# Second mixture of experts: gate and up rows dealt to the partitions in fours

## The chip, the cores and the metric

One core of one Trainium2 chip runs the whole program in one launch. The metric is the device time of one execution in microseconds (us). Beside it stands the time of one profiled execution, whose trace is read here.

## The reference, cut to what matters

The program runs two stacks of blocks over 256 tokens of 1024 features in float32. The second stack has two layers, and each ends in the mixture that this change touches (`hier_moe`, inputs whose names end in `_2`). It has 16 experts in 4 groups of 4. Every token chooses one group and two experts in it:

```python
a = silu(einsum('td,edf->tef', t, w_gate)) * einsum('td,edf->tef', t, w_up)   # d = 1024, f = 256
y = einsum('tef,efd->td', a * comb[:, :, None], w_down)
```

`w_gate` and `w_up` of an expert are 1024 x 256 (1 MB each, rows of 1 KB), `w_down` is 256 x 1024 (rows of 4 KB). The 48 MB of weights of a layer are read once. The sum over d may be taken in any order, as long as weights and tokens use the same one.

## The kernel before, in words

**Stages.** The first stack (with a larger mixture, `od_moe_gu` and `od_moe_down`) takes about the first two thirds of the span. Then come, for each layer of the second stack, an attention mixer and the mixture. Everything is written out by hand: each engine has one program in order, and semaphores join them.

**Blocks.** Weights come in blocks of 2 MB through a ring of seven slots (`ring`, 16 KB in each partition). SyncE issues the transfers (line 1258, in `load`), in the order of a list of blocks. Before it loads block i + 7 into a slot, it waits until TensorE has read block i (`free_slot`). For the second mixtures it also waits for the ranking of the four groups by their number of tokens (`order_ready`, line 1301), since the group that a block belongs to is chosen at run time.

**Order in a layer.** A group is two pairs of experts, c0 and c1. Each pair needs a gate block, an up block and a down block; a gate block holds the gate weights of two experts side by side, loaded by two DMAs of 1 MB. The 24 blocks of a layer are numbered here b0 to b23: gate and up of pair 0 (b0, b1), gate and up of pair 1 (b2, b3), down of pair 0 (b4); then for each further group gate and up of its c0, the down block of the group before, gate and up of its c1, down of its c0; at the end the last down block. So the gate and up blocks of the third group's second pair are b14 and b15, those of the fourth group b17, b18 and b20, b21, and the last two down blocks b22 and b23.

**Layout.** A slot holds a gate block as eight chunks of 512 columns: chunk k has row 128 k + p of both experts in partition p, 256 columns of each. So every run that a DMA moves is one row, 1 KB. A down block has rows of 1024, so its runs are 4 KB.

**Tokens.** For each layer TensorE turns the normalised tokens into rows (line 1974), ScalarE copies the four results into `xn_tok` (line 2630), and TensorE gathers the tokens of each group out of it, 128 features at a time (line 2002), into `x_group`.

**Products.** Groups are ranked by tokens. The two largest are computed in tiles of 32 rows, four at a time (`triple_one`, `triple_two`, `triple_three`; the matmuls are in `tile_stream`, line 1752), down products at line 1856. The two smaller ones are computed in tiles of 64 rows (`group_pair`, line 1806; `group_down`, line 1819). A transpose of the hidden values (lines 1842 and 1730) stands in the middle of the next product, and the scatter back to the tokens (lines 1914 and 1916) behind it. The moving operand of gate and up matmuls is a chunk of 512 columns out of the ring, the stationary one 32 or 64 tokens of `x_group`.

Where a group has more tokens than its tiles hold (96 in the first two, 64 in the others), a branch (lines 1308, 2051) computes the rest. It did not run here.

Of the kernel before, what the change touches and what calls it, by code (L numbers as in the profile page):

```python
# [30 lines left out]
P = 128  # L31
# [3 lines left out]
KD = D // P  # L35
# [9 lines left out]
E2, E2_FF = 16, 256  # L45
# [49 lines left out]


GROUP_CAP = 3 * QP
GROUP_CAPS = [GROUP_CAP, GROUP_CAP, HP, HP]
GROUP_MOST = [T, T // 2, T // 3, T // 4]
GROUP_MORE = [(g, at, min(P, n - at + 1 & ~1)) for g, (n, cap) in enumerate(zip(GROUP_MOST, GROUP_CAPS)) for at in range(cap, n, P)]  # L100
# [113 lines left out]
def stacked_blocks_kernel(nc, A, consts_dram, counts_dram, slots_dram, out):  # L214
    with ExitStack() as ctx:
# [297 lines left out]
        def slot_data(b):  # L513

            return ring[:, b.slot, :] if b.slot < SLOTS else zf

        def kblk(b):

# [456 lines left out]
        def experts(l, h_at):  # L975
# [20 lines left out]
            st.loads = []  # L996

            def by_group(W):
                return W[l].rearrange("(g e) (k p) n -> g e p k n", e=EPG, p=P)

            def pair(W, n):

                return [(lambda j: lambda b: lambda g: (kblk(b)[:, :, j * E2_FF:(j + 1) * E2_FF],
                                                        by_group(W)[g, 2 * n + j]))(j) for j in range(2)]

            def gate_up(x, c):
                n = c.c - 2 * x.i
# [232 lines left out]
        @block_.sync  # L1240
        def _(sp):
            def released(b):
                if b.release is not None:
                    sp.wait_ge(*b.release)
                for tile in b.other_tiles:
                    sp.wait_ge(*tile)

            def free_slot(i):

                if blocks[i].earlier is not None:  # L1250
                    released(blocks[i].earlier)

            def load(i, expert=None):
                b = blocks[i]
                for l in b.loads:
                    place = l(b)
                    dst, src = place if isinstance(place, tuple) else place(expert)
                    sp.dma_start(dst, src).then_inc(slot_landed[b.slot], 16)

            sp.dma_start(x_tok[:, 0, :], A["x"][0][0:P, :]).then_inc(tokens_landed, 16)  # L1260
            for dst, src in SMALL[:ROWS_BY_SP]:
                sp.dma_start(dst, src).then_inc(rows_landed, 16)
            for i in range(SLOTS):
                load(i)
            for dst, src in LATE:
                sp.dma_start(dst, src).then_inc(late_landed, 16)
            for i in range(SLOTS, moe1_first):
                free_slot(i)
                load(i)
            for i in range(*moe1[0].blocks):  # L1270
                free_slot(i)
                load(i, 0)
            sp.wait_ge(order_ready, 1)
            for st in moe1[1:]:
                expert = sp.value_load(order[0:1, st.rank:st.rank + 1], min_val=0, max_val=E1 - 1)
                for i in range(*st.blocks):
                    free_slot(i)
                    load(i, expert)

            sp.wait_ge(excess_ready, 1)  # L1280
            with sp.If(sp.value_load(order[0:1, E1:E1 + 1], min_val=0, max_val=T) > CAPS[0]):
                for b in blocks[moe1_last - SLOTS - 1:moe1_last]:
                    released(b)
                for m, (rank, at, w) in enumerate(MORE):
                    expert = sp.value_load(order[0:1, rank:rank + 1], min_val=0, max_val=E1 - 1)
                    with sp.Fori(0, N1) as s:
                        sp.wait_ge(more_down, s + (m * N1 + 1))
                        for slot_i, src in enumerate((gu1_steps[expert, 0, s], gu1_steps[expert, 1, s], dn1_steps[expert, s])):
                            dst = (ring[:, slot_i, :].rearrange("p (k n) -> p k n", n=WBLK if slot_i < 2 else D))
                            sp.dma_start(dst, src).then_inc(more_landed, 16)  # L1290
                sp.wait_ge(more_added, 4 * len(MORE))
            at = moe1_last
            for st in moe2:
                group = None
                for i in range(at, st.blocks_end):
                    if i == moe1_last + 1:
                        sp.wait_ge(spread_ready, twin.spread + 1)
                    if i == moe2[0].blocks_end + 2:
                        sp.wait_ge(spread_ready, od2.norm.spread + 1)
                    if i == st.blocks_begin:  # L1300
                        sp.wait_ge(order_ready, st.route.order + 1)
                        group = [sp.value_load(order2[0:1, st.l * EG + g:st.l * EG + g + 1], min_val=0, max_val=EG - 1)
                                 for g in range(EG)]
                    free_slot(i)
                    load(i, group[blocks[i].group] if i >= st.blocks_begin else None)
                at = st.blocks_end
                sp.wait_ge(most_ready, st.route.most + 1)
                with sp.If(sp.value_load(most2[0:1, st.l:st.l + 1], min_val=0, max_val=T) > GROUP_CAP):
                    for b in blocks[at - SLOTS:at]:
                        released(b)  # L1310
                    for m, (g, at_slot, w) in enumerate(GROUP_MORE):
                        of = sp.value_load(order2[0:1, st.l * EG + g:st.l * EG + g + 1], min_val=0, max_val=EG - 1)
                        for n in range(2):
                            if n:
                                sp.wait_ge(excess_product[st.l], 9 * m + 5)
                            elif m:
                                sp.wait_ge(excess_product[st.l], 9 * m - 1)
                            for slot_i, W in enumerate((A["moe_w_gate_2"], A["moe_w_up_2"])):
                                dst = ring[:, slot_i, :].rearrange("p (k n) -> p k n", k=KD)
                                for j in range(2):  # L1320
                                    src = st.by_group(W)[of, 2 * n + j]
                                    sp.dma_start(dst[:, :, j * E2_FF:(j + 1) * E2_FF], src).then_inc(excess_landed[st.l], 16)
                            sp.dma_start(ring[:, 2, :].rearrange("p (k n) -> p k n", n=D), st.down_rows[of, n])\
                                .then_inc(excess_landed[st.l], 16)
                    sp.wait_ge(excess_made[st.l], 5 * len(GROUP_MORE))
            for i in range(at, len(blocks)):
                free_slot(i)
                load(i)
            sp.wait_ge(rows_out[1], 2)
            sp.dma_start(out[0][P:2 * P, :], x_tok[:, 1, :]).then_inc(out_landed, 16)  # L1330
            sp.wait_ge(out_landed, 32)
# [12 lines left out]
        def _(pe):  # L1344
# [404 lines left out]

            def tile_stream(f, j, at, b, k, src=xn):  # L1750

                return nc.tensor.matmul(PSB[f.b][j * QP:(j + 1) * QP, :], src[:, k, at:at + QP], kblk(b)[:, k, :],  # L1752
                                        start=k == 0, stop=k == KD - 1)

            def triple_one(x, turn, src=xn):
# [42 lines left out]
            def group_pair(x, c, middle):  # L1798

                landed(c.gate)  # L1800
                landed(c.up)
                ps = open_bank(c.pair.fill)
                for k in range(KD):
                    if k == KD // 2:
                        middle()
                    ends = [nc.tensor.matmul(ps[half * HP:(half + 1) * HP, :], x_group[x.i][:, k, 0:HP], kblk(b)[:, k, :],  # L1806
                                             start=k == 0, stop=k == KD - 1) for half, b in enumerate((c.gate, c.up))]
                for mm, (full, n) in zip(ends, c.pair.tile):
                    mm.then_inc(full, 1)
# [236 lines left out]
            def pe_excess(st):  # L2046
# [4 lines left out]
                with pe.If(pe.value_load(most2[0:1, l:l + 1], min_val=0, max_val=T) > GROUP_CAP):  # L2051
                    for m, (g, at, w) in enumerate(GROUP_MORE):
# [9 lines left out]
                        for n in range(2):  # L2062
                            pe.wait_ge(excess_landed[l], 160 * m + 80 * (n + 1))
                            pe.wait_ge(made, 5 * m + 2 + n)
                            for half in range(2):
                                w_half = ring[:, half, :].rearrange("p (k n) -> p k n", k=KD)
                                for k in range(KD):
                                    mm = nc.tensor.matmul(PSB[half][0:w, :], xn[:, k, 0:w], w_half[:, k, :],
                                                          start=k == 0, stop=k == KD - 1)
                            mm.then_inc(done, 1)  # L2070
                            pe.wait_ge(made, 5 * m + 3 + n)
# [343 lines left out]
        def _(act):  # L2415
# [210 lines left out]
            def act_tokens_by_row(fills, of=None):  # L2626
                for i, f in enumerate(fills):
                    to = xn_tok[:, i // 2, i % 2 * 512:(i % 2 + 1) * 512]
                    if of is None:
                        nc.scalar.copy(to, full(f)).then_inc(xtok_ready, 1)  # L2630
                    else:
                        act.wait_ge(root_ready, of.root + 1)
                        nc.scalar.activation(to, full(f), ACT.Copy, scale=roots[:, 1, i // 2:i // 2 + 1]).then_inc(xtok_ready, 1)
# [1211 lines left out]
```

## Time and profile before

| | us |
|---|---|
| median of 3 runs | 2366.76 |
| lowest and highest of them | 2365.67, 2369.34 |
| the profiled execution, its own time | 2362.55 |
| its span, first to last instruction | 2360.9 |
| TensorE busy in the span | 2265.6 (96%) |
| VectorE, ScalarE busy | 691.4, 365.9 |
| mean granted clock of TensorE | 0.979 of full speed |

A busy TensorE is not the same as one that never waits: 96% is an average over stages, and the two mixtures of the second stack, at 1818 to 1972 us and at 2189 to 2344 us of the span, have to be read by themselves. Times in rows below count from the start of the span. "PE" is TensorE, "PEld" its weight loads, "DVE" VectorE, "ACT" ScalarE, "SPq" the queue of SyncE.

### The profile page before, as it was taken

Reading aid. Unit: us, or ns where it says so; the run is one execution under the profiler, and the core shown is the slowest. Engines: PE = TensorE matmul, PEld = TensorE weight load, DVE = VectorE, ACT = ScalarE, POOL = GpSimd, SP = SyncE. Lnnn points to the kernel's source line nnn. Section 1 sums busy time; section 2 is a strip of 40 time slices with the busy share of each in tenths; the row PEclk is TensorE's granted clock in tenths of the full one; section 3 lists DMA queues with packets and bytes.
Section 4 is the critical chain, followed back from the end, with each engine's and each line's share of the span. In section 5 each row is a group of like instructions: output and inputs, shape, how many; then the busy total and the mean of one; then the engine's idle time right before and its main releaser. Section 6 shows DMA issues by size and latency. Waiting matters only on the chain.

```text
span 2360.9 us, 32972 instructions
## 1 busy us (share of the span) xinstructions
PE 2265.6 (96%) x14022; PEld 1317.0 (56%) x14022; DVE 691.4 (29%) x1539; ACT 365.9 (15%) x795; POOL 1.2 (0%) x9
## 2 busy tenths in 40 slices
PE   7899999999989999999999999999989989989997
PEld 6777888888577333333333333335756336856433
DVE  2575222149766101101010101012243122273222
ACT  2102100010212111111111011112032101153211
POOL 0000000000000000000000000000000000000000
PEclk9899999999999999999999999998999999999998
DMA  9498254474266999999999999996501998800995
GB/s 324 175 366 314 72 209 183 147 265 167 105 221 257 349 364 399 408 405 408 405 387 405 409 405 409 399 391 262 184 1 61 364 365 277 187 1 6 315 364 195
DMA packets 281391, 644.99 MB, mean 273 GB/s; under 512 B 14715, under 2 KB 99985, under 8 KB 281233
## 3 DMA queue, kind: packets, MB, share of 16 engines
q1 hardware_dynamic: 278588, 638.16, 73.3%
q10 hardware_dynamic: 2645, 4.59, 0.6%
q8 instruction: 116, 1.90, 0.3%
q14 instruction: 42, 0.34, 0.0%
HBM read 641.67 MB, written 1.05 MB: 272 GB/s over the span
## 4 chain that ended last, share of the span: by engine, by line
PE 88%; DVE 6%; issue 2%; ACT 2%; DMA 1%; SPq 1%; ACTq 0%; DVEq 0%
PE bank L1715 21%; PE bank L1363 20%; PE bank L1856 9%; PE bank L1638 6%; PE bank L1752 4%; PE bank L1652 3%; PE bank L1806 3%; DVE att L3636 3%; PE bank L1403 2%; PE bank L1744 2%; PE bank L1916 1%; PE bank L1875 1%; PE bank L1819 1%; DMA ring<-od_moe_down 1%; PE bank L1914 1%
## 5 line engine op out<-in xcount | busy, mean ns | idle before, releaser
L1715 PE MATMUL bank<-ring,xn 128*32 128x512 f32 (+1 forms) x3552 | 467.5, 593 | 0.0
L1363 PE MATMUL bank<-xn,ring 128*128 128x256 f32 x1920 | 423.3, 382 | 2.4 <-issue 1.0
L1363 PEld LDWEIGHTS bank<-xn,ring 128*128 128x128 f32 x1920 | 366.4, 192 | 56.2 <-issue 6.4
L1715 PEld LDWEIGHTS bank<-ring,xn 128*32 128x32 f32 (+1 forms) x3552 | 140.2, 114 | 303.2 <-issue 301.9
L1856 PE MATMUL bank<-ring,att 128*32 128x512 f32 x1824 | 205.2, 593 | 0.0
L3194 DVE TENSOR_TENSOR sq<-att,bank 32x512 f32<-32x512 f32 x70 | 48.0, 686 | 409.1 <-ACT att L2582 407.5
L1638 PE MATMUL bank<-xn,ring 128*128 128x256 f32 x640 | 138.9, 379 | 0.0
L1856 PEld LDWEIGHTS bank<-ring,att 128*32 128x32 f32 x1824 | 59.5, 110 | 133.1 <-issue 132.8
L1638 PEld LDWEIGHTS bank<-xn,ring 128*128 128x128 f32 x640 | 121.6, 190 | 16.5
L2582 ACT ACTIVATE att<-bank 64x512 f32<-64x512 f32 (+1 forms) x115 | 67.7, 589 | 355.7 <-PE bank L1715 290.6
L2571 ACT COPY att<-bank 128x384 f32<-128x384 f32 (+1 forms) x72 | 29.0, 438 | 522.5 <-PE bank L1842 342.6
L3267 DVE SCALAR_TENSOR_TENSOR att<-ring,cs,att 128x512 f32<-128x512 f32 x133 | 100.0, 752 | 4.7
L3636 DVE SCALAR_TENSOR_TENSOR att<-z,cols,att 128x256 f32<-128x256 f32 x240 | 95.5, 475 | 0.1
L1752 PE MATMUL bank<-ring,xn 128*32 128x512 f32 x768 | 86.2, 601 | 0.5 <-issue 0.5
L1652 PE MATMUL bank<-att,ring 128*128 128x256 f32 x320 | 70.3, 380 | 0.0
L1715 PE MATMUL bank<-z,xn 128*32 128x512 f32 (+1 forms) x480 | 67.8, 594 | 0.5 <-ACT xn L2618 0.5
L1744 PE MATMUL bank<-ring,att 128*64 128x512 f32 x304 | 67.2, 593 | 0.6 <-DMA ring<-od_moe_down 0.6
L1652 PEld LDWEIGHTS bank<-att,ring 128*128 128x128 f32 x320 | 60.4, 190 | 8.0
L3186 DVE TENSOR_TENSOR sq<-att,bank 64x512 f32<-64x512 f32 x21 | 14.5, 692 | 159.0 <-ACT att L2582 159.0
L2424 ACT ACTIVATE sq<-h 128x512 f32<-128x512 f32 x44 | 27.4, 629 | 200.2 <-DVE h L3041 88.4
L3172 DVE TENSOR_TENSOR att<-att,bank 128x256 f32<-128x256 f32 x22 | 9.2, 420 | 157.6 <-ACT att L2562 157.6
L1752 PEld LDWEIGHTS bank<-ring,xn 128*32 128x32 f32 x768 | 23.8, 111 | 56.4 <-issue 55.8
(393 smaller groups left out, 2088.5 us busy)
## 6 DMA issues: line engine op xcount, KB each, us to landing
ring<-od_moe_gu SPq DMA_DIRECT2D x196, 1024.0 KB, 15.1
ring<-od_moe_down SPq DMA_DIRECT2D x49, 2048.0 KB, 16.6
ring<-ada_w SPq DMA_DIRECT2D x24, 2048.0 KB, 9.3
ring<-moe_w_gate SPq DMA_DIRECT2D x32, 1024.0 KB, 13.8
ring<-moe_w_up SPq DMA_DIRECT2D x32, 1024.0 KB, 12.0
ring<-moe_w_down SPq DMA_DIRECT2D x16, 2048.0 KB, 14.0
z<-od_moe_gu SPq DMA_DIRECT2D x28, 1024.0 KB, 12.4
ring<-ev_w_in SPq DMA_DIRECT2D x10, 2048.0 KB, 20.2
```

The lines of the kernel that those rows point to most:

```text
L1363: mm = nc.tensor.matmul(ps[:, c * T:(c + 1) * T], kblk(b)[:, k, u * T + c * P:u * T + (c + 1) * P], x[:, k, :], start=k == 0, stop=k == KD ...
L1638: mm = nc.tensor.matmul(ps[:, half * T:(half + 1) * T], kblk(b)[:, k, j * P:(j + 1) * P], src[:, k, :], start=k == 0, stop=k == KD - 1)
L1652: mm = nc.tensor.matmul(PSB[st.y[m // 2].b][:, m % 2 * T:(m % 2 + 1) * T], rblk(x.down)[:, j, m * P:(m + 1) * P], hid[:, s % 2, j, :], sta ...
L1715: mm = nc.tensor.matmul(PSB[r.fill.b][j * w:(j + 1) * w, :], xn[:, k, at:at + w], rows_[:, half, c * WBLK:(c + 1) * WBLK], start=k == 0, s ...
L1744: low, high = [nc.tensor.matmul(PSB[f.b][half * HP:(half + 1) * HP, :], hid[:, s % 2, j, 0:HP], rblk(x.down)[:, j, half * 512:(half + 1) * ...
L1752: return nc.tensor.matmul(PSB[f.b][j * QP:(j + 1) * QP, :], src[:, k, at:at + QP], kblk(b)[:, k, :], start=k == 0, stop=k == KD - 1)
L1806: ends = [nc.tensor.matmul(ps[half * HP:(half + 1) * HP, :], x_group[x.i][:, k, 0:HP], kblk(b)[:, k, :], start=k == 0, stop=k == KD - 1) f ...
L1856: return nc.tensor.matmul(PSB[f.b][t * QP:(t + 1) * QP, :], hid[:, x.c % 2, j, at:at + QP], rblk(x.down)[:, j, half * 512:(half + 1) * 512 ...
L2582: nc.scalar.activation(to, PSB[r.fill.b][rows_, :], ACT.Silu).then_inc(sg_ready, 1)
L3194: return nc.vector.tensor_tensor(to, sgx, up, ALU.mult)
L3267: ins = nc.vector.scalar_tensor_tensor(y, w[:, k, :], cs[:, k:k + 1], y, ALU.mult, ALU.add)
L3636: ins = nc.vector.scalar_tensor_tensor(y, x, w, y, ALU.mult, ALU.add)
```

## The change

Gate and up rows of the second mixtures are laid out by a new rule. Row 512 k + 4 p + r goes to partition p, chunk 4 k + r (k of two, r of four), and the two experts of a block stand behind each other in the slot, 8 KB each, where they were interleaved. The four rows 4 p to 4 p + 3 are contiguous in memory and in the slot, so a DMA moves runs of 4 KB. There are as many DMAs as before, of the same sizes. The moving operand of a gate or up matmul is then two stretches of 256 columns, 8 KB apart, where it was one of 512. So that features meet their weights, ScalarE's copies into `xn_tok` write feature 512 k + 4 p + r to column 512 k + 128 r + p: neighbours in the source lie 512 B apart in the destination. Nothing else is altered; the router, which reads `xn`, keeps its order.

```diff
+DEAL = 4
...
+        def by_expert(x):
+
+            return x.rearrange("p (e k n) -> p k e n", e=2, k=KD)
+
+        def dealt(x, e):
+
+            return x[:, :, e, :].rearrange("p (k r) n -> p k (r n)", r=DEAL)
+
+        def eblk(b):
+
+            return by_expert(slot_data(b))
...
             def by_group(W):
-                return W[l].rearrange("(g e) (k p) n -> g e p k n", e=EPG, p=P)
+                return W[l].rearrange("(g e) (k p r) n -> g e p k (r n)", e=EPG, p=P, r=DEAL)
...
-                return [(lambda j: lambda b: lambda g: (kblk(b)[:, :, j * E2_FF:(j + 1) * E2_FF],
-                                                        by_group(W)[g, 2 * n + j]))(j) for j in range(2)]
+                return [(lambda j: lambda b: lambda g: (dealt(eblk(b), j), by_group(W)[g, 2 * n + j]))(j) for j in range(2)]
...
-                return nc.tensor.matmul(PSB[f.b][j * QP:(j + 1) * QP, :], src[:, k, at:at + QP], kblk(b)[:, k, :],
+                return nc.tensor.matmul(PSB[f.b][j * QP:(j + 1) * QP, :], src[:, k, at:at + QP], eblk(b)[:, k],
...
-                    ends = [nc.tensor.matmul(ps[half * HP:(half + 1) * HP, :], x_group[x.i][:, k, 0:HP], kblk(b)[:, k, :],
+                    ends = [nc.tensor.matmul(ps[half * HP:(half + 1) * HP, :], x_group[x.i][:, k, 0:HP], eblk(b)[:, k],
...
-                        nc.scalar.copy(to, full(f)).then_inc(xtok_ready, 1)
+                        dealt_to = xn_tok[:, i // 2, :].rearrange("q (k r p) -> q k p r", r=DEAL, p=P)
+                        features = [slice(0, KD // DEAL // 2), slice(KD // DEAL // 2, KD // DEAL)][i % 2]
+                        nc.scalar.copy(dealt_to[:, features], full(f).rearrange("q (k p r) -> q k p r", r=DEAL, p=P))\
+                            .then_inc(xtok_ready, 1)
```

The branch for groups with more tokens than their tiles hold is changed in the same way.

## Rows read from the trace of the kernel before

**Rows 1.** The page: busy time of each engine, its share of the span, instructions.

```profile
PE 2265.6 (96%) x14022; PEld 1317.0 (56%) x14022; DVE 691.4 (29%) x1539; ACT 365.9 (15%) x795; POOL 1.2 (0%) x9
```

**Rows 2.** Three stretches: busy time of each engine, then granted clock, DMA share, GB/s.

```profile
1060.00:1120.00 60.00, 60.00 (x512) 22.68 (x512) 8.45 (x15) 7.88 (x16) 0.00 (x0) 1.00 1.03 409
1860.00:1890.00 30.00, 29.77 (x276) 9.20 (x272) 3.55 (x8) 4.47 (x8) 0.00 (x0) 1.00 1.07 369
...
1949.00:1953.00 4.00, 3.79 (x12) 1.45 (x14) 0.00 (x0) 0.00 (x0) 0.00 (x0) 0.61 1.03 412
```

**Rows 3.** Transfers, 1821 to 1963 us: GB/s in 40 slices of 3.55 us, packets.

```profile
GB/s 352 351 353 347 350 347 374 404 354 348 348 383 399 352 347 348 392 393 347 350 351 397 383 353 347 355 405 374 348 348 361 408 367 348 348 371 408 410 397 387
DMA packets 38245, 52.20 MB, mean 368 GB/s; under 512 B 646, under 2 KB 33178, under 8 KB 38235
```

**Rows 4.** TensorE in order of time, layer 0: start, duration, work [idle before it].

```profile
1863.66 3.64 PE L1752 MATMUL bank<-ring,xn 128*32 128x512 f32 x32 [0.23 <-issue]
...
1876.32 10.48 PE L1752 MATMUL bank<-ring,xn 128*32 128x512 f32 x96
...
1908.26 5.36 PE L1856 MATMUL bank<-ring,att 128*32 128x512 f32 x48
1914.97 3.65 PE L1806 MATMUL bank<-ring,memT 128*64 128x512 f32 x16 [1.36 <-issue]
...
1932.15 5.35 PE L1806 MATMUL bank<-ring,z 128*64 128x512 f32 x16 [2.21 <-issue]
...
1941.30 3.60 PE L1819 MATMUL bank<-ring,att 128*64 128x512 f32 x16
1949.21 5.35 PE L1806 MATMUL bank<-ring,z 128*64 128x512 f32 x16 [4.30 <-issue]
```

**Rows 5.** Line 1258: the two DMAs of b21, issue times and landing.

```profile
L1258 SPq DMA_DIRECT2D ring<-moe_w_up x2: 2787/3146/3505, 1933.7 to 1937.4; - x2
DMA to landing us min/median/max: 11.8/12.1/12.5
```

**Rows 6.** Line 1258: the layer's first two DMAs, issued into an empty queue.

```profile
L1258 SPq DMA_DIRECT2D ring<-moe_w_gate x2: 388/414/439, 1818.5 to 1819.0; - x2
...
DMA to landing us min/median/max: 5.7/7.2/8.6
```

**Rows 7.** TensorE in order of time, layer 1: the matmuls behind an idle stretch.

```profile
2235.04 3.64 PE L1752 MATMUL bank<-ring,xn 128*32 128x512 f32 x32 [0.29 <-issue]
...
2286.43 3.65 PE L1806 MATMUL bank<-ring,memT 128*64 128x512 f32 x16 [1.44 <-issue]
...
2303.60 5.35 PE L1806 MATMUL bank<-ring,z 128*64 128x512 f32 x16 [2.21 <-issue]
...
2320.67 5.96 PE L1806 MATMUL bank<-ring,z 128*64 128x512 f32 x16 [4.32 <-issue]
```

**Rows 8.** Around the copies into `xn_tok`, layer 0: ScalarE.

```profile
1811.69 1.56 ACT L2630 COPY vtok<-bank 128x512 f32<-128x512 f32 x3 [0.23 <-PE bank L1974]
...
1814.56 0.33 ACT L2642 ACTIVATE rt<-rt 128x8 f32<-128x8 f32 x2
```

**Rows 9.** The same stretch: TensorE's gather, and VectorE's first use of the exponentials.

```profile
1817.79 10.56 PE L2002 MATMUL bank<-z,vtok 128*128 128x384 f32 x32 [2.15 <-issue]
...
1818.55 0.28 DVE L3291 TENSOR_TENSOR sq<-rt 128x128 f32<-128x128 f32 x1
```

**Rows 10.** The page, matmuls with one stretch as moving operand: busy us, mean ns.

```profile
L1363 PE MATMUL bank<-xn,ring 128*128 128x256 f32 x1920 | 423.3, 382 | 2.4 <-issue 1.0
...
L1856 PE MATMUL bank<-ring,att 128*32 128x512 f32 x1824 | 205.2, 593 | 0.0
```

**Rows 11.** Line 2002: moving operand in four stretches of 96. ns min/median/max.

```profile
L2002 PE MATMUL bank<-z,vtok x64: 486/486/561, 1817.8 to 2199.2; 128*128 128x384 f32 x64
```

**Rows 12.** VectorE by line and shape: a read with a stride of 64 B, and one without.

```profile
L3762 DVE TENSOR_TENSOR memT<-z,cols 128x240 f32<-128x240 f32 x8 | 3.9, 545 | 0.0
...
L3600 DVE TENSOR_TENSOR att<-att,kT 128x256 f32<-128x256 f32 x4 | 1.7, 424 | 0.1
```

More of the change, by code:

```diff
@@ L1318, in _ @@
                             for slot_i, W in enumerate((A["moe_w_gate_2"], A["moe_w_up_2"])):
-                                dst = ring[:, slot_i, :].rearrange("p (k n) -> p k n", k=KD)
+                                dst = by_expert(ring[:, slot_i, :])
                                 for j in range(2):
                                     src = st.by_group(W)[of, 2 * n + j]
-                                    sp.dma_start(dst[:, :, j * E2_FF:(j + 1) * E2_FF], src).then_inc(excess_landed[st.l], 16)
+                                    sp.dma_start(dealt(dst, j), src).then_inc(excess_landed[st.l], 16)
                             sp.dma_start(ring[:, 2, :].rearrange("p (k n) -> p k n", n=D), st.down_rows[of, n])\
@@ L2065, in pe_excess @@
                             for half in range(2):
-                                w_half = ring[:, half, :].rearrange("p (k n) -> p k n", k=KD)
+                                w_half = by_expert(ring[:, half, :])
                                 for k in range(KD):
-                                    mm = nc.tensor.matmul(PSB[half][0:w, :], xn[:, k, 0:w], w_half[:, k, :],
+                                    mm = nc.tensor.matmul(PSB[half][0:w, :], xn[:, k, 0:w], w_half[:, k],
                                                           start=k == 0, stop=k == KD - 1)
```

## The prediction, on record before the changed kernel was run

> **What bounds the kernel now.** I read the page first: TensorE is busy for 96% of the span [rows 1]. By that average, faster transfers would be worth nothing. The change touches only the mixtures of the second stack, so I asked next for the stretches there, beside one of the first mixture. In both the 16 DMA engines are busy without a break (shares of 1.03 and 1.07 [rows 2]), but they move 409 GB/s in the one and 369 in the other. The slices of the transfer view show why: inside the second mixture the rate alternates between about 348 and about 402 [rows 3]. Of 38,245 packets there 33,178 are under 2 KB. Those are the 1 KB runs of gate and up (16 blocks x 2,048 runs = 32,768), and the high slices are the down blocks between them, in runs of 4 KB. So a gate or up block (2.097 MB) takes 2.097 / 348 = 6.03 us, a down block 2.097 / 402 = 5.22 us.
>
> Then TensorE in order of time. In layer 0 it is idle ahead of four products of gate and up, for 0.23, 1.36, 2.21 and 4.30 us, and the trace names no engine as the releaser ("issue") [rows 4]. It is the transfers: the second DMA of b21 was issued at 1937.4 and landed 11.8 us later, at 1949.2 [rows 5], and the product that reads it starts at 1949.21. Three blocks are 2 x 6.03 + 5.22 = 17.3 us, which puts b18 at 1931.9 and b15 at 1914.6, where the products behind the other waits start at 1932.15 and 1914.97. So the first half of a mixture runs at TensorE's pace, and the second waits for gate and up blocks. Layer 1 repeats it: 0.29, 1.44, 2.21 and 4.32 us [rows 7].
>
> Two waits also cost clock. After idle stretches of 2.21 and 4.30 us the next 16 matmuls take 5.35 us, where the same work takes 3.65 us after one of 1.36 us [rows 4]: the mean granted clock of 1949 to 1953 us is 0.61 [rows 2], a mix of the two levels 1.2 and 2.4 GHz. That is 1.70 us each, in layer 1 1.70 and 2.31 us [rows 7].
>
> **The change part by part.**
>
> *The transfers.* Gate and up in runs of 4 KB have the shape of a down block, on both sides: contiguous rows of 4 KB in memory, 4 KB in the slot. I take its 402 GB/s: each of 16 blocks is 6.03 - 5.22 = 0.81 us shorter. b21 has all 16 of them at or before it, so it lands 16 x 0.81 = 13.0 us earlier, at 1936.2. b18 (14 of them) lands at 1931.9 - 11.3 = 1920.6, b15 (12) at 1914.6 - 9.7 = 1904.9. The bounds of the rate are 348 (no gain) and 409, the first mixture's [rows 2].
>
> *When TensorE wants them.* Without the waits TensorE comes to b15's product 0.23 us earlier than its end of work at 1913.6, thus at 1913.4; to b18's at 1929.9 - 0.23 - 1.36 = 1928.3; to b21's at 1944.9 - 0.23 - 1.36 - 2.21 - 1.70 = 1939.4. The three blocks are there 8.5, 7.7 and 3.2 us ahead. In layer 1 TensorE wants b21 at 2320.67 - 4.32 - 2.21 - 1.70 - 1.44 - 0.29 = 2310.7 and gets it at 2320.7 - 13.0 = 2307.7, 3.0 us ahead. All waits go, and the slow clock behind them. Gain in layer 0: 0.23 + 1.36 + 2.21 + 4.30 + 2 x 1.70 = 11.5 us; in layer 1: 0.29 + 1.44 + 2.21 + 4.32 + 1.70 + 2.31 = 12.3 us. The margin of 3 us also says how firm this is: it takes 22 blocks of 5.22 + 0.14 us, 391 GB/s, until a wait comes back. Beyond b21 only two down blocks are left, 5.2 and 10.4 us behind it; the first is read after the whole product of b21 (two times 3.65 us) and a scatter, the second later still. They have more room, and the rest of the layer hangs on TensorE and moves with it.
>
> *The slots.* A faster stream meets a ring of seven. Block i + 7 may be issued only once block i is read. With the new pace block b13 is due to flow at 1821.4 + 13 x 5.22 = 1889.3 (1821.4 is b21's landing less 16 x 6.03 + 6 x 5.22 us), and its slot is that of b6, the first up block of the second group, read until the end of that group's second round at about 1883.5 (64 of the 96 matmuls from 1876.32 on [rows 4]). Room: 5.8 us. All other blocks have 7 us or more. A first DMA of 1 MB into an empty queue landed after 5.7 us [rows 6], of which 2.6 are its bytes at 402 GB/s, so about 3.1 us of room is enough. No gap; cost nothing.
>
> *SyncE.* As many DMAs, each with a quarter of the runs. Its issue times of 2.8 and 3.5 us [rows 5] are spent with over 11 us of transfers queued ahead. They cost nothing now and can only shrink.
>
> *The moving operand in two stretches.* Line 2002 has four stretches of 96 columns in each matmul and takes 486 ns [rows 11]. Matmuls with one stretch take 382 ns for 256 columns and 593 for 512 [rows 10]; between them, 384 columns would take 488. Three jumps cost nothing that shows, so one costs nothing. This edit has no cover: gate and up matmuls are about 6 x 7.14 + 4 x 7.3 = 72 us of each layer, on the path. Bounds: 0, and a second start (rival 3).
>
> *The copies.* Four copies per layer now write with a step of 512 B. Three of them take 1.56 us now. The last ends at 1813.25, and the gather that reads them starts at 1817.79 [rows 8, 9], held by VectorE's slot masks; the exponentials behind them on ScalarE end at 1814.9 and are first used at 1818.55. The trace has no such write. The nearest row is a read of VectorE with a step of 64 B: 545 ns for 240 columns, where 256 contiguous ones take 424 [rows 12], some 0.57 ns more for each column. On 512 columns that is 0.3 us a copy, 1.2 us for four, inside the 3.65 us of room of the exponentials and the 4.5 us of the gather. Even a doubled copy (2.4 us for four) is hidden; the cost starts above 0.9 us more per copy. I take 0, with an upper bound of 1 us per layer.
>
> The Trainium skill ("Advanced Engine Details and Errata", SBUF Cachelines) says that accesses to SBUF lose speed when each falls into another line of 16 bytes, which speaks against these copies; it gives no size. The read with a 64 B step agrees in direction, and by it the sum stays the same because of the room.
>
> **Sum.** 11.5 + 12.3 = 23.8 us. The profiled execution took 2362.55 us, so 2338.8 by its own time. It ran 4.2 us below the median of the three runs, 2366.76; against that the forecast is 2366.8 - 23.8 = 2343.0 us, 1.0% faster.
>
> **The rivals.**
>
> 1. *Only half of the gap closes.* The 402 of a down block might owe something to its place: a block of long runs between blocks of short ones. If gate and up came halfway (5.63 us a block), b21 would land 6.4 us earlier, at 1942.8 where TensorE wants it at 1939.4. A wait of 3.4 us stays with its slow clock: 5.1 us back, 6.4 us gained. In layer 1 3.6 + 2.3 back, 6.4 gained. Time 2366.8 - 12.8 = 2354.0. Against it: the first mixture holds 409 over 60 us [rows 2].
>
> The Trainium skill ("DMA: Bandwidth & Descriptors", Why small descriptors are slow) gives each packet a fixed overhead of about 3 cycles on 32-byte beats, so 35 beats for 1 KB and 131 for 4 KB. By that page the gain would be an estimated 4 x 35 / 131 = 1.07, not the 1.155 between the two rates here; worked through, that lands near this rival.
>
> 2. *The rate does not follow the runs.* If gate and up stay at 348 for another reason (where their pages lie in memory, say), nothing moves: 2366.8, no change. Against it: both kinds of blocks are read by the same queue, in the same stretch, into the same ring.
>
> 3. *A second stretch costs TensorE a second start: slower.* 512 columns take 593 ns and 256 take 382, so a start is some 171 ns beyond the columns. If it were paid once more in each step and could not be hidden, the 96 four-tile steps and 64 two-tile steps of a layer would cost 160 x 0.17 = 27 us more; less the 11.9 us of waits that go, 15 us a layer: 2397. It decides from 12 / 160 = 0.075 us a step on. Against it speak rows 10 and 11.
>
> **Chances.** The forecast (18 to 26 us gained) 0.73; rival 1 and what lies between it and the forecast or just below 0.15; rival 2 0.05; rival 3, with very slow copies, 0.07. A difference within 0.2%, 4.7 us, can hardly be told from none; that leaves faster 0.88, same 0.05, slower 0.07. By its own bounds the forecast lies in 2339 to 2348. With half of the gap it is 2354, so the range goes to 2355 and leaves out rivals 2 and 3; its low end adds 2 us for the runs' own spread.
>
> **What would show it.** Right: in the second mixtures the packets under 2 KB fall to a few hundred, every slice is at 400 or more, TensorE's idle stretches marked "issue" ahead of lines 1752 and 1806 are gone and their first 16 matmuls take 3.65 us, the mean of line 1806 stays at 592 ns, and from 1913 us on everything is earlier by 1.6, then 5.5, then 11.5 us. SyncE would then wait for slots in the first half. Wrong: matmuls of lines 1752 and 1806 longer than 593 ns, slices under 391 GB/s, gaps in the DMA share, or a gather that waits for ScalarE. Copies longer than 0.52 us apiece would be a miss without price.

## The result, and the profile after

| us | before | changed |
|---|---|---|
| median, runs | 2366.51, 4 | 2339.61, 4 |
| lowest and highest | 2365.67, 2369.34 | 2335.14, 2342.93 |
| the profiled execution | 2362.55 | 2335.14 |
| its span | 2360.9 | 2333.5 |

The ratio is 0.9883, with a 95% interval of 0.9862 to 0.9904: 27.7 us faster (22.7 to 32.7), where 23.8 us were forecast. Two more measurements of the same kernel gave 0.9865 (0.9850 to 0.9880) and 0.9878 (0.9861 to 0.9894), so 27.7 to 32 us. The first interval alone still holds the forecast's 23.8 us; those of the two repeats (28.4 to 35.5 and 25.1 to 32.9 us) don't, and all three values lie beyond the 18 to 26 us that the forecast spanned. The mechanism is the forecast one, its size was too small by about 4 us or more.

Transfers of the changed kernel, 1821 to 1963 us of its span: GB/s in 40 slices and packets [answers to rows 3].

```profile
GB/s 0 245 410 417 410 410 412 407 407 408 408 410 408 410 407 405 410 408 408 406 410 413 407 410 405 412 408 408 412 407 412 405 410 407 412 406 390 388 389 87
DMA packets 15019, 54.68 MB, mean 385 GB/s; under 512 B 672, under 2 KB 672, under 8 KB 15008
```

Runs of 1 KB are gone, and the 348 with them: gate, up and down flow alike at some 409. The layer's transfers begin at about 1825 us, in the second slice; the slices under 400 at the end, from 1949 us on, are for the most part weights of the next stage, behind the last down block (landed at about 1951).

TensorE of the changed kernel in order of time, layer 0 [rows 4].

```profile
1823.55 10.56 PE L2014 MATMUL bank<-z,vtok 128*128 128x384 f32 x32 [2.15 <-issue]
1833.94 3.63 PE L2024 MATMUL bank<-kT,z 128*128 128x2 f32 x32
1837.43 2.03 PE L1974 MATMUL bank<-const,kT 128*128 128x128 f32 x16
1839.40 17.37 PE L1764 MATMUL bank<-ring,xn 128*32 128x512 f32 x160
...
1910.36 5.36 PE L1868 MATMUL bank<-ring,att 128*32 128x512 f32 x48
1915.64 3.65 PE L1818 MATMUL bank<-ring,memT 128*64 128x512 f32 x16
...
1926.95 3.65 PE L1831 MATMUL bank<-ring,att 128*64 128x512 f32 x16
1930.43 3.60 PE L1818 MATMUL bank<-ring,z 128*64 128x512 f32 x16
...
1937.84 3.60 PE L1831 MATMUL bank<-ring,att 128*64 128x512 f32 x16
1941.27 3.60 PE L1818 MATMUL bank<-ring,z 128*64 128x512 f32 x16
...
1961.54 2.96 PE L1926 MATMUL bank<-kT,memT 64*128 64x256 f32 x16 [0.76 <-ACT memT L2662]
```

(Lines are 12 higher than before: 1764 is the old 1752, 1818 the old 1806, 1926 the old 1914.) No product of gate and up has idle time ahead of it, and the 5.35 us stretches of slow clock are 3.60 us. No matmul of the product line takes longer for its two stretches. Its mean on the page is 593 ns; line 1752 had 601 before, with slow clock in it:

```profile
L1764 PE MATMUL bank<-ring,xn 128*32 128x512 f32 x768 | 84.8, 593 | 0.0
...
L1752 PE MATMUL bank<-ring,xn 128*32 128x512 f32 x768 | 86.2, 601 | 0.5 <-issue 0.5
```

The same places in the trace of the kernel before, which the account below needs.

```profile
1828.19 4.78 PE L2012 MATMUL bank<-kT,z 128*128 128x2 f32 x32
1832.83 3.76 PE L1962 MATMUL bank<-const,kT 128*128 128x128 f32 x16
1836.52 17.70 PE L1752 MATMUL bank<-ring,xn 128*32 128x512 f32 x160
...
1971.22 2.96 PE L1914 MATMUL bank<-kT,memT 64*128 64x256 f32 x16 [0.76 <-ACT memT L2647]
```

**The account.** Cut a mixture at three starts: the gather (1817.79 [rows 9], now 1823.55), the first product of gate and up (1836.52, now 1839.40), the last scatter (1971.22, now 1961.54). From gather to last scatter it was 153.4 us and is 138.0. In layer 1 it was 154.2 (from 2189.09 to 2343.29) and is 138.0. The mixtures give 31.7 us. Outside them the changed execution loses 4.3: it reaches the first gather 5.8 us later, over code that is the same in both (in the other twelve traces that gather starts between 1818.8 and 1823.2 us, so most of this is the one early execution of the kernel before), and wins 0.7 us between the mixtures and 0.8 us at the end. 31.7 - 4.3 = 27.4, the difference of the spans.

My forecast, put in this way, was a mixture of 153.4 - 11.5 = 141.9 and 154.2 - 12.3 = 141.9 us. The miss is 3.9 us a layer, in 141.9 against 138.0. In layer 0, 2.9 of it lie between gather and first product (18.73 us before, 15.85 now), 0.3 in the first 160 matmuls, 0.7 at the four places where a wait went. In layer 1 it is 2.2, 1.0 (18.42 us for the 160 matmuls, now 17.37) and 0.7. So in each layer 3.2 us of the miss lie ahead of the first wait.

The length of 153.4 us has two parts. The product of b21 starts when the transfers deliver it, 131.4 us after the gather (1949.21 - 1817.79), and 22.0 us of TensorE's work follow up to the last scatter. In the changed kernel TensorE comes to that product by itself after 117.7 us, and 20.3 us follow: 13.7 us less ahead of it, 1.7 us of slow clock less behind it.

### The profile page after: what moved, and what is told of

Its sections match the earlier page's. It is cut to its first block, busy times and chain, and to the rows that moved or that the text cites. A ratio compares the mean times of both kernels' runs of the same rounds, so it can differ in the third digit from the quotient of the medians.

```text
span 2333.5 us, 32972 instructions
## 1 busy us (share of the span) xinstructions
PE 2254.7 (97%) x14022; PEld 1313.0 (56%) x14022; DVE 691.6 (30%) x1539; ACT 369.3 (16%) x795; POOL 1.2 (0%) x9
## 4 chain that ended last, share of the span: by engine, by line
PE 90%; DVE 6%; ACT 2%; issue 1%; ACTq 0%; DVEq 0%
PE bank L1727 23%; PE bank L1375 20%; PE bank L1868 10%; PE bank L1650 7%; PE bank L1764 4%; PE bank L1756 3%; PE bank L1664 3%; DVE att L3651 3%; PE bank L1818 2%; PE bank L1415 2%; PE bank L1928 1%; PE bank L1887 1%; PE bank L1831 1%; PE bank L1926 1%; PE bank L2014 1%
## 5 line engine op out<-in xcount | busy, mean ns | idle before, releaser
L1650 PEld LDWEIGHTS bank<-xn,ring 128*128 128x128 f32 x640 | 121.6, 190 | 16.5
L2436 ACT ACTIVATE sq<-h 128x512 f32<-128x512 f32 x44 | 27.4, 629 | 200.8 <-DVE h L3056 88.4
L3056 DVE SCALAR_TENSOR_TENSOR h<-bank,mod,h 128x256 f32<-128x256 f32 x80 | 32.8, 477 | 73.9 <-PE bank L1375 56.3
## 6 DMA issues: line engine op xcount, KB each, us to landing
z<-od_moe_gu SPq DMA_DIRECT2D x28, 1024.0 KB, 12.3
```

Of the source, the lines that this page charges most:

```text
L1650: mm = nc.tensor.matmul(ps[:, half * T:(half + 1) * T], kblk(b)[:, k, j * P:(j + 1) * P], src[:, k, :], start=k == 0, stop=k == KD - 1)
```

## The experiments

Edits are against the changed kernel, those of before_half and before_delay against the kernel before. A ratio compares a kernel with the kernel before as measured beside it. All lengths below run from the start of the gather to the start of the last scatter, in us, for layer 0 and layer 1; "routing" is the part up to the first product.

| kernel | routing | length | median | ratio to before |
|---|---|---|---|---|
| before | 18.7, 18.1 | 153.4, 154.2 | 2366.5 | |
| before_again | 16.9, 16.3 | 153.3, 153.4 | 2365.6 (one) | |
| deal1 | 16.9, 18.1 | 153.5, 153.6 | 2367.0 | 1.0000 (0.9991 to 1.0009) |
| slot_1k | 17.4, 18.1 | 156.0, 155.0 | 2367.9 | 1.0008 (0.9999 to 1.0017) |
| before_delay | 21.3, 21.3 | 153.5, 154.2 | 2368.6 | 1.0012 (1.0003 to 1.0021) |
| changed | 15.9, 15.9 | 138.0, 138.0 | 2339.6 | 0.9883 (0.9862 to 0.9904) |
| after_again | 16.5, 18.5 | 139.6, 141.2 | 2336.3 | 0.9865 (0.9850 to 0.9880) |
| after_third | 15.8, 15.9 | 138.0, 138.0 | 2337.1 | 0.9878 (0.9861 to 0.9894) |
| deal2 | 18.6, 16.3 | 142.5, 142.7 | 2342.3 | 0.9891 (0.9875 to 0.9906) |
| deal8 | 15.9, 15.9 | 138.0, 138.0 | 2337.2 | 0.9874 (0.9858 to 0.9890) |
| before_half | 15.9, 15.9 | 138.0, 138.0 | 2336.6 | 0.9883 (0.9865 to 0.9901) |
| after_delay | 19.7, 19.7 | 141.8, 141.8 | 2346.3 | 0.9911 (0.9897 to 0.9924) |
| plain_copies | 15.8, 15.9 | 138.0, 138.0 | 2334.4 | 0.9870 (0.9848 to 0.9893) |
| spread_late | 15.0, 14.0 | 141.0, 138.2 | 2336.1 | 0.9868 (0.9851 to 0.9884) |

**after_again, after_third, before_again: the same kernels once more.** No edit.

> The changed kernel once more, unaltered. Theory A (part of the gain beyond the forecast is granted clock, which differs between executions whatever the kernel): the median is 23 to 28 us below the kernel before, and the stretch from the start of the gather to the first product of gate and up (15.9 us in both layers of the first trace of the changed kernel, 18.7 and 18.1 us before) is free to come out at 16 or at 18 to 19 us. Theory B (the change itself keeps the clock up there): 15.9 us in both layers again. In both, no idle stretch ahead of gate and up products, 408 GB/s.

> The kernel before once more, for a second trace. Theory A: the four waits per layer are as in the first trace (0.2 to 0.3, 1.4, 2.2, 4.3 us), while stretches of slow clock lie elsewhere or have other lengths; the stretch from gather to first product may be 16 us in one layer. Theory B: 18 to 19 us in both layers.

> The changed kernel a third time, to stand beside the next three on one chip. If its mixtures are set by TensorE and the clock of small matmuls differs between executions, both lengths from gather to last scatter lie between 138.0 and 141.5 us and the time between 2333 and 2343.

The kernel before had routings of 18.7, 18.1, 16.9 and 16.3 us in its two traces, and its mixtures were 153.3 to 154.2 all the same. The time won in the routing went into waits. Layer 0 of before_again, in order of time: the wait of 0.23 us in the first trace [rows 4] is 1.55 us here, b1 is waited for too, and b21's product starts 131.3 us after the gather at 1821.83.

```profile
1838.75 18.17 PE L1752 MATMUL bank<-ring,xn 128*32 128x512 f32 x160 [0.44 <-DMA ring<-moe_w_up]
...
1867.68 3.64 PE L1752 MATMUL bank<-ring,xn 128*32 128x512 f32 x32 [1.55 <-issue]
...
1953.15 5.29 PE L1806 MATMUL bank<-ring,z 128*64 128x512 f32 x16 [4.39 <-issue]
```

The changed kernel had 15.9 four times, 16.5 and 18.5, and there the length moved with it: 138.0, 139.6, 141.2. It moved by a little more than the routing, since the first 160 matmuls took 18.4 and 18.0 us in after_again, where they take 17.4 at full clock. Its median is 31.1 us below the kernel before, more than the 23 to 28 expected. What differs in the routing is the granted clock. Two stretches in the kernel before (clock in the third column from the end):

```profile
1830.00:1832.00 2.00, 2.00 (x14) 2.00 (x13) 0.00 (x0) 0.00 (x0) 0.00 (x0) 0.60 1.08 351
1832.00:1834.00 2.00, 2.00 (x10) 2.00 (x11) 0.17 (x1) 0.00 (x0) 0.00 (x0) 0.50 1.11 350
```

And at the same work in the changed kernel's first trace:

```profile
1834.00:1836.00 2.00, 2.00 (x21) 2.00 (x19) 0.00 (x0) 0.60 (x3) 0.00 (x0) 1.00 1.02 406
1836.00:1838.00 2.00, 2.00 (x20) 2.00 (x20) 0.17 (x1) 0.00 (x0) 0.00 (x0) 1.00 1.02 412
```

In the kernel before the clock went from its higher level to its lower one while TensorE was busy without a break; its last idle stretch was the 2.15 us ahead of the gather, and the changed kernel had the same one.

TensorE in order of time in after_again, layer 1:

```profile
2188.97 4.50 PE L2024 MATMUL bank<-kT,z 128*128 128x2 f32 x32
2193.33 3.76 PE L1974 MATMUL bank<-const,kT 128*128 128x128 f32 x16
```

The 3.76 us for these 16 small matmuls are those of the kernel before, not the 2.03 us of the first trace of the changed one. In between, they took 2.65 us in layer 0 of after_again, and 2.60 and 2.48 us in before_again: a part at either level. So both programs get either clock, and theory B as put is wrong. But the low level is not equally frequent. Of the ten routings traced in kernels with the full bytes in 1 KB packets (before, before_again, deal1, slot_1k, before_delay) six have the 3.76 us, of twelve in kernels where TensorE sets the length and nothing was added (the changed one three times, deal8, plain_copies, before_half) one has. These two groups were formed after the results; of the ten, one has the 2.03 us of full clock (layer 0 of deal1) and three lie between. before_half streams packets of 1 KB there too and kept its clock in both layers, which speaks against the packets flowing beside it, but two routings don't settle it. Whether and how the clock is tied to the kernel stays open. (Not every routing of 16.3 to 16.9 us has the same reason: in layer 0 of deal1 the clock is full, 2.03 us, and the first product waits 0.97 us for b1; those of 16.3 and 16.5 have no such wait and 2.48 to 2.65 us for the 16 matmuls.)

**deal1: everything but the long runs.**

```diff
-DEAL = 4
+DEAL = 1
```

> DEAL = 1: experts behind each other in the slot and a moving operand in two stretches of 256, but runs of 1 KB and copies in natural order. If the runs are the cause: waits of about 0.3, 1.4, 2.2 and 4.3 us are back in both layers, about 349 GB/s in slices of gate and up, matmuls of both product lines 593 ns, and the time of the kernel before within 3 us. If the order in the slot were the cause: 15 to 27 us faster than before. If two stretches cost TensorE something that the shorter transfers had covered: matmuls over 600 ns and a time above the kernel before. Theory A on the clock: the stretch from gather to first product can be 16 or 18 to 19 us; theory B: 18 to 19 us in both layers.

Ratio 1.0000. Slices of gate and up at 348 to 353, waits back (in layer 0 not at the expected places: 0.97 us for b1, then 2.32, 2.09 and 4.33), matmuls of line 1764 at 592 ns in median. Its waits by line (total, times, longest), over both layers from 1830 us on:

```profile
PE bank L1818 <- issue: 14.3, 5, 4.3
PE bank L1764 <- issue: 2.7, 2, 2.3
```

The order in the slot and the two stretches are neutral, so what is left of the change is the runs and the sorted copies; plain_copies, below, takes the copies out. The runs are the cause.

**slot_1k: long runs on the memory side alone.**

```diff
-            return x.rearrange("p (e k n) -> p k e n", e=2, k=KD)
+            return x.rearrange("p (k e n) -> p k e n", e=2, k=KD)
...
-        def dealt(x, e):
-            return x[:, :, e, :].rearrange("p (k r) n -> p k (r n)", r=DEAL)
+        def dealt(x, e, k):
+            return x[:, k * DEAL:(k + 1) * DEAL, e, :]
```

> Rows dealt in fours in memory (4 KB contiguous on that side), tokens sorted likewise, but the two experts interleaved in the slot as in the kernel before, so the slot side has pieces of 1 KB; each DMA is cut in two of 512 KB, since the pattern has one dimension too many. If a run has to be contiguous on both sides: packets of 1 KB, 348 GB/s in gate and up, the waits of the kernel before, 2362 to 2372. If the memory side alone counts: packets of 4 KB or a rate near 408, 2333 to 2343.

The memory side is the changed kernel's, the slot side the old one; each DMA of 1 MB is two of 512 KB here. No gain: its waits ahead of b21's product are 7.20 and 6.10 us, longer than before, and the median is within 0.2%. Its transfers, 1836 to 1960 us:

```profile
GB/s 350 348 347 349 384 397 363 349 348 354 401 390 350 349 354 373 407 366 349 349 354 395 394 352 351 349 366 407 374 348 348 352 389 400 355 344 349 365 407 407
DMA packets 34113, 45.51 MB, mean 367 GB/s; under 512 B 1032, under 2 KB 30356, under 8 KB 34104
```

deal1 is the other way round, 8 KB contiguous in the slot and rows of 1 KB in memory, and has packets of 1 KB too (33,407 of 37,703 are under 2 KB between 1821 and 1963 us). In both, the packet is as long as the shorter side allows.

**deal2 and deal8: runs of 2 and 8 KB.**

```diff
-DEAL = 4
+DEAL = 2
```

For 8, the copies are written as `"q (r p) -> q p r"`, half of the p for each.

> DEAL = 2: runs of 2 KB. If each run costs a fixed time beside its bytes, 348 GB/s at 1 KB and 408 at 4 KB give 8.9 ns a run and some 386 GB/s at 2 KB, 0.3 us more per gate or up block than at 4 KB. b21 landed 0.8 us before its use in the changed kernel (1940.5, used at 1941.3), so it would come 16 x 0.3 = 5 us later and leave a wait of about 4 us with 1.7 us of slow clock behind it in each layer: 8 to 12 us slower than the changed kernel, 14 to 20 us faster than before. Rival: 2 KB runs already flow at over 400 GB/s, then it is within 3 us of the changed kernel.

> DEAL = 8: row 8 p + r in partition p, so one run of 8 KB per partition and DMA. Theory: TensorE sets the length at 4 KB already, so longer runs give nothing even if they flow faster: within 3 us of the changed kernel, lengths of 138 to 141.5 us. If transfers still limited it, 2 us or more faster.

Transfers of deal2, 1835 to 1960 us:

```profile
GB/s 386 385 388 391 408 396 389 388 389 404 401 385 388 387 404 402 389 387 385 406 404 389 388 385 398 408 389 387 387 399 406 391 386 387 393 414 408 407 387 387
```

TensorE behind its longer wait, in layer 1:

```profile
2304.77 3.65 PE L1818 MATMUL bank<-ring,z 128*64 128x512 f32 x16 [2.83 <-issue]
```

The rate is the forecast 386. The waits ahead of b21's product are 1.03 and 2.83 us, where 4 were expected, and no slow clock follows (3.65 us for 16 matmuls). Between medians on one chip it is 6.0 us slower than the changed kernel; 8 to 12 were expected. In layer 0 the wait is short because TensorE came late: the routing took 18.6 us. b21's product starts 122.1 and 122.3 us after the gather, where the changed kernel's starts after 117.7. The busy time of deal8 in one stretch, GB/s last, shows 416:

```profile
1860.00:1890.00 30.00, 30.00 (x280) 9.24 (x276) 4.31 (x10) 4.47 (x8) 0.00 (x0) 1.00 1.02 416
```

and gained nothing, with lengths of 138.0: at 4 KB the transfers no longer set the end.

**before_half: less to move, in the old layout.**

```diff
-(kblk(b)[:, :, j * E2_FF:(j + 1) * E2_FF], by_group(W)[g, 2 * n + j])
+(kblk(b)[:, 0:KD // 2, j * E2_FF:(j + 1) * E2_FF], by_group(W)[g, 2 * n + j][:, 0:KD // 2])
```

> The kernel before, but each gate and up DMA loads only the first four of its eight chunks (the products read old values for the others, so a part of the computation is left out). Runs stay at 1 KB and TensorE's work is the same. Theory: with 16.8 MB less to move in each layer TensorE sets the length, 138 to 141 us a mixture, as in the changed kernel, and the time is 2333 to 2343. If the changed kernel had gained by something else than transfer time (the order in the slot, the copies), this one would stay above it by more than 5 us.

It leaves half of the gate and up weights unloaded, so its output is not that of the program. Lengths of 138.0 and 138.0, and a ratio of 0.9883 beside 0.9883, 0.9865 and 0.9878 of the changed kernel. Its stretch from 1860 to 1890 us, with DMA share and GB/s last, moves 246 GB/s, and TensorE is busy throughout:

```profile
1860.00:1890.00 30.00, 30.00 (x280) 9.04 (x269) 3.14 (x7) 4.48 (x8) 0.00 (x0) 1.00 0.70 246
```

So 138.0 us is TensorE's own length at full clock, in either layout.

**before_delay and after_delay: more work for TensorE.**

```diff
                 pe_spread(r.pos_fills, g_slot)
+                busy(st.norm.idle, 10)
```

> The kernel before, with 10 dummy matmuls (of zeros, 128x512 in bf16; 7 of them take 1.67 us in the trace, so 2.4 us) ahead of the first product of each mixture. Theory: the length from the start of the gather to the last scatter is set by the transfers there (153.3 to 153.6 us in the four mixtures traced in kernels with 1 KB runs and no other change to it, whatever the clock of the routing), so 2.4 us more of TensorE's work disappear in the waits: length unchanged, time within 1.5 us of the kernel before. If instead my forecast's way of counting were right (TensorE's work and its waits simply add up), 4.8 us slower.

> The changed kernel with the same 10 dummy matmuls in each mixture. Theory: TensorE sets the length there, so each layer gets 2.4 us longer, 140.4 us at full clock where it was 138.0, and the time is 4 to 5 us above the changed kernel, 23 to 27 us below the kernel before. If transfers or slots still set the length, nothing or less than 2 us is seen. If the dummies keep the clock up in the routing, up to 2.9 us a layer come back: then no more than 0 to 2 us slower, and the routing stretch shows no slow clock.

The ten dummies took 3.5 and 3.4 us in after_delay, and 2.8 and 3.4 in before_delay, not 2.4; the granted clock beside them was 0.65 in layer 0 of after_delay, so they didn't hold it up. Here in after_delay, in order of time:

```profile
1837.90 3.52 PE L1446 MATMUL bank<-zeros 128*128 128x512 bf16 x10
```

In the kernel before they vanish in the waits: lengths of 153.5 and 154.2, with routings of 21.3 us. The first two waits are gone, the third is 1.96 us, and b21's product starts 131.5 us after the gather at 1821.31:

```profile
1935.76 5.35 PE L1806 MATMUL bank<-ring,z 128*64 128x512 f32 x16 [1.96 <-issue]
...
1952.82 5.35 PE L1806 MATMUL bank<-ring,z 128*64 128x512 f32 x16 [4.30 <-issue]
```

Over the eight mixtures of before, before_again, deal1 and before_delay that start is 131.3 to 131.6 us after the gather, for routings of 16.3 to 21.3 us. In the changed kernel the dummies are paid in full, 141.8 in both layers, 3.8 more than 138.0; the rest beside the dummies' own time comes from the 16 small matmuls ahead of them, 2.55 us where they had 2.03. The medians agree with the lengths (7.7 us by them; 2346.3 against 2336 to 2340), but the 4 to 5 us expected were too few, by the dummies' clock. For before_delay the ratio says 2.8 us slower (0.7 to 5.0), more than I allowed; the lengths don't show it, and where it comes from stays open.

**plain_copies: tokens in natural order.**

```diff
-                        nc.scalar.copy(dealt_to[:, features], full(f).rearrange("q (k p r) -> q k p r", r=DEAL, p=P))\
+                        nc.scalar.copy(to, full(f))\
```

> The changed kernel with the copies of the tokens in natural order, 0.59 us where the sorted ones take 1.09 us (features then don't meet their weights: the order of the features is what is left out). Theory: the copies lie in the shadow of VectorE's slot masks, so the time is that of the changed kernel within 3 us, and the gather starts behind the same 2.15 us wait. If they cost time: 4 us or more faster (8 copies of 0.5 us).

The sorted copies of the changed kernel, by line (ns min/median/max):

```profile
L2644 ACT COPY vtok<-bank x8: 1064/1094/1107, 1816.6 to 2174.4; 128x512 f32<-128x512 f32 x8
```

And those of plain_copies:

```profile
L2642 ACT COPY vtok<-bank x8: 586/589/605, 1816.0 to 2173.1; 128x512 f32<-128x512 f32 x8
```

0.5 us less for each copy, and the same lengths; the gather stands behind the same 2.15 us. What it leaves out is the match of features and weights, not any work. The ratios don't differ beyond their intervals.

**spread_late: a try for a faster version.**

```diff
-                pe_spread(r.pos_fills, g_slot)
...
                         triple_one(x, prev.c[1] if prev is not None else None, src)
+                        if prev is None:
+                            pe_spread(r.pos_fills, g_slot)
```

> The changed kernel with the 16 small matmuls that spread the tokens' places (2.0 us at full clock, 3.8 at the low one) moved from ahead of the first product of a mixture to behind its first round. TensorE's work is the same, but fewer small matmuls stand in a row. Theory: the first product is then wanted 2 us earlier, at about 1837.4 in the first trace's time, where b1 landed at 1838.2, so a wait of about 1 us appears instead and little is won: 0 to 3 us faster than the changed kernel, by the slow clock that is spared. If the place of the small matmuls has no effect on the clock: the same within 1.5 us.

TensorE in layer 0, in order of time:

```profile
1833.82 8.77 PE L1764 MATMUL bank<-ring,xn 128*32 128x512 f32 x64 [0.98 <-DMA ring<-moe_w_up]
1842.52 2.05 PE L1974 MATMUL bank<-const,kT 128*128 128x128 f32 x16
```

The spreads ran at full clock, but the first product now waits 0.98 us for b1 and starts at the low clock (8.77 us for 64 matmuls, 7.07 in layer 1). Nothing that can be measured is won.

## Why the prediction came out as it did

- *The transfers bound the second half of a mixture*: right. before_half takes the bytes away and gets the changed kernel's length; deal1 keeps the layout and not the runs, and gets nothing.
- *Runs of 4 KB flow at 402*: right, a little low; 409 was measured, the first mixture's rate [rows 2]. A down block of 5.2 us fills at most one slice of 3.55 us whole, so slices beside runs of 1 KB can read low.
- *All four waits go, and the slow clock behind two of them*: right in both layers. But b21 was not 3.2 us ahead. Its second DMA left at 1923.8 and landed 16.7 us later, at 1940.5, for a product that starts at 1941.27. The issue in the changed kernel:

```profile
L1270 SPq DMA_DIRECT2D ring<-moe_w_up x1: 1012/1012/1012, 1923.8 to 1923.8; - x1
DMA to landing us min/median/max: 16.7/16.7/16.7
```

  The loads start with the ranking, the products with the routing, and the routing had become 2.9 us shorter. The margin was 0.8 us in place of 3.2, which is why deal2 shows waits.
- *The sum of 11.5 and 12.3 us*: the step that failed. It took away the waits and the slow clock behind two of them, and so put the rest of TensorE's time in that trace at what it would need anyway. But ahead of the first wait TensorE had run at low clock, 3.2 us in each layer (18.7 and 18.1 us of routing, 17.7 and 18.4 for the first 160 matmuls, where full clock gives 15.9 and 17.4). The sum put that term at nothing. It had no price, because the waits behind it were as much shorter: before_again has routings 1.8 us shorter and waits longer instead, at the same length. The right difference is between two lengths, 153.4 set by transfers and 138.0 to 141.2 set by TensorE, thus 12 to 16 us a layer. What I forecast, 141.9, is close to after_again's layer with the slow routing. That the other traced layers of the changed kernel came out at full clock or nearly is a part of the gain that the change may not own, since nothing here shows what sets this clock; layout alone is sure of some 12 us a layer. The smaller part of the miss, 0.2 us for each wait that went, is the overlap of one group of matmuls with the next (1926.95 + 3.65 is 1930.60, the next starts at 1930.43).
- *Slots and SyncE*: right, no cost. SyncE now waits for slots, as said, and the DMA share stays above 1.
- *Two stretches as moving operand cost nothing*: right (deal1, and 593 ns on the page).
- *The copies*: cost 0 was right, their size was not. I took 0.3 us more each from a read of VectorE with a step (the two rows give 0.61 ns a column, not the 0.57 I wrote); it was 0.5, just under the doubled copy that I had allowed for.
- *Rival 1, half of the gap*: fell, 409 against 348 is 1.18. The rule of the Trainium skill ("DMA: Bandwidth & Descriptors", Why small descriptors are slow) gave an estimated 1.07; the measurement decides. *Rival 2* and *rival 3* fell with the trace and with deal1.

## What to carry to other kernels

When a stage passes from one bound to another, don't subtract the visible waits: find the length that each bound would give by itself (here by taking half of the bytes away), and take the difference. Slow clock and small delays ahead of a wait are free while the wait stands, and are paid as soon as it goes. For weights with rows of 1 KB, deal neighbouring rows to one partition, contiguous on both sides, and pay with a sorted copy where another engine covers it.

## What the runs showed of the hardware

- Rates in full streams: 348 GB/s in runs of 1 KB, 386 at 2 KB, 409 at 4 KB, 416 at 8 KB. With 16 engines, 348 and 409 mean 47 ns for 1 KB and 160 ns for 4 KB on one engine, so about 9 ns a run beside 38 ns a KB; that gives 386 at 2 KB and about 420 at 8 KB.
- A copy of ScalarE that writes neighbours 512 B apart took 1.09 us for 512 columns, a contiguous one 0.59: 1 ns a column more. "Advanced Engine Details and Errata", SBUF Cachelines, in the Trainium skill names such a penalty; here is its size for this copy.
- The same 16 small matmuls took 2.03 us, 3.76 us or something between in different executions of one program, more often 3.76 in kernels whose mixtures wait for transfers; why is open.
- Neither the length of a wait nor an earlier wait decides by itself whether low clock follows. After 2.21 us in the kernel before (with 1.36 us a few products earlier) and after 1.96 us in before_delay (with no wait for transfers ahead of it) the next 16 matmuls took 5.35 us. After 2.83 us in deal2, and after 2.21 us in slot_1k with 1.64 us a few products earlier, they took 3.65 us. Here the last of these:

```profile
1937.89 3.65 PE L1820 MATMUL bank<-ring,z 128*64 128x512 f32 x16 [2.21 <-issue]
```
